# Down weights of the experts requested from ScalarE's queue, and the matmul order of the expert blocks

## The reference

```
hid = silu(xb @ w_gate_e[e]) * (xb @ w_up_e[e])     # 1024 -> 256
y   = hid @ w_down_e[e]                             # 256 -> 1024
```

## Time and profile before

| what | us |
|---|---|
| three runs, median (lowest to highest) | 2059.25 (2058.33 to 2060.5) |
| profiled execution, device time | 2059.05 |
| profiled execution, span | 2056.0 |

### The profile page before, as it was taken

One profiled execution on the slowest core, in us unless ns is written; L12 is line 12 of the kernel. 1 busy time (PEld: TensorE's weight loads), 2 busy tenths in 40 slices (PEclk: granted clock), 3 DMA queues, 4 the chain that ended last, 5 costly groups with the idle time before them and its releaser, 6 DMA issues.

```text
span 2056.0 us, 23309 instructions
## 1 busy us (share of the span) xinstructions
PE 1977.9 (96%) x9524; PEld 1411.7 (69%) x9524; DVE 1004.5 (49%) x1599; ACT 746.0 (36%) x1283; POOL 220.5 (11%) x271
## 2 busy tenths in 40 slices
PE   7999999999999999999999999999999998988888
PEld 6877788888888888888888886678886333323233
DVE  4376533445766642568988738664434211111113
ACT  5343332234444431466555533662333111111110
POOL 2000000002000000201112114110011221111100
PEclk9999999999999999999999999999999999999999
DMA  7331222243222242323332221112279999999998
GB/s 265 106 123 62 79 86 82 103 148 129 103 103 89 96 144 103 131 86 108 128 118 95 94 103 62 42 62 103 101 317 338 416 409 421 421 421 421 422 423 331
DMA packets 64059, 379.90 MB, mean 185 GB/s; under 512 B 13624, under 2 KB 13880, under 8 KB 32464
## 3 DMA queue, kind: packets, MB, share of 16 engines
q1 hardware_dynamic: 45792, 339.23, 42.8%
q0 software_dynamic: 17584, 38.09, 5.3%
q10 hardware_dynamic: 576, 1.09, 0.2%
HBM read 377.80 MB, written 27.89 MB: 197 GB/s over the span
## 4 chain that ended last, share of the span: by engine, by line
PE 76%; DMA 14%; DVE 5%; ACT 1%; SPq 1%; POOL 1%; issue 1%; DVEq 0%; POOLq 0%; ACTq 0%
PE PS L534 19%; PE PS L535 18%; PE PS L536 18%; DMA AR<-in_wexp 12%; PE PS L1301 6%; PE PS L995 3%; PE PS L1330 2%; SPq L3132 1%; DMA AR<-x2d 1%; PE PS L900 1%; DVE AR L1753 1%; PE PS L1047 1%; PE PS L1077 1%; PE PS L1279 1%; DVE rf L1379 1%
## 5 line engine op out<-in xcount | busy, mean ns | idle before, releaser
L534 PE MATMUL PS<-rf,rf 128*128 128x512 f32 (+1 forms) x1944 | 752.8, 387 | 5.3 <-DVE rf L1379 5.3
L536 PE MATMUL PS<-rf,rf 128*128 128x512 f32 (+1 forms) x1944 | 741.9, 382 | 0.0
L535 PE MATMUL PS<-rf,rf 128*128 128x512 f32 (+1 forms) x1944 | 741.2, 381 | 0.0
L1379 DVE TENSOR_TENSOR rf<-AR,rf 128x1024 fp32r<-128x1024 f32 (+1 forms) x228 | 286.0, 1260 | 335.2 <-ACT rf L2321 335.2
L534 PEld LDWEIGHTS PS<-rf,rf 128*128 128x128 f32 x1944 | 366.3, 188 | 81.8 <-DVE rf L1379 7.3
L536 PEld LDWEIGHTS PS<-rf,rf 128*128 128x128 f32 x1944 | 366.0, 188 | 70.6
L535 PEld LDWEIGHTS PS<-rf,rf 128*128 128x128 f32 x1944 | 366.6, 189 | 68.1 <-issue 1.2
L2321 ACT ACTIVATE rf<-AR 128x1024 fp32r<-128x1024 f32 (+1 forms) x228 | 245.2, 1084 | 258.1 <-PE PS L536 202.9
L1301 PE MATMUL PS<-AR 128*64 128x512 f32 x1012 | 266.2, 635 | 48.2 <-DMA AR<-in_wexp 47.9
L1301 PEld LDWEIGHTS PS<-AR 128*64 128x64 f32 x1012 | 81.8, 146 | 222.7 <-issue 154.5
L2246 DVE COPY AR<-PS 128x256 f32<-128x256 f32 x32 | 13.6, 425 | 316.1 <-PE PS L1313 316.1
(11 more groups left out here) (349 smaller groups left out, 1802.4 us busy)
## 6 DMA issues: line engine op xcount, KB each, us to landing
AR<-in_wpack SPq DMA_DIRECT2D x123, 1024.0 KB, 5.0
AR<-in_wexp SPq DMA_DIRECT2D x64, 1024.0 KB, 32.3
AR<-in_wexp SPq DMA_DIRECT2D x28, 2048.0 KB, 33.4
AR<-in_wexp SPq DMA_DIRECT2D x26, 1536.0 KB, 32.1
AR<-in_wexp SPq DMA_DIRECT2D x63, 512.0 KB, 20.9
AR<-acud POOLq DMA_DIRECT2D x16, 512.0 KB, 4.8
AR<-ya SPq DMA_DIRECT2D x4, 1024.0 KB, 8.2
bvec<-bv POOLq DMA_DIRECT2D x1, 2560.0 KB, 16.0
```

What stands on the lines that cost most here:

```text
L534: e.i.matmul(o, ws[0], xs[0], start=start, stop=False)
L535: e.i.matmul(o, ws[0], xs[1], start=False, stop=False)
L536: return e.i.matmul(o, ws[1], xs[0], start=False, stop=stop)
L1379: e.i.tensor_tensor(rounded(p.place + p.width, p.width), src, rounded(p.place, p.width).bitcast(F32), ALU.subtract).then_inc(*tick("w_lo", ...
```

## The change

Four things change.

1. Down weights of experts 6 to 63 are no longer in SP's list. ACT asks for them: after it has evicted block b (`rows_out`, L2866) it issues the two transfers for block b + 3, each 1 MB. SP keeps gate/up weights (and down weights of experts 0 to 5).
2. These transfers count on semaphores of their own (`da`), for which `downs` waits.
3. From block 2 on PE no longer runs gates one block ahead: the order is `gates(b)`, `turned_rows(b+1)`, `hidden(b)`, `downs(b)`. Blocks 0 and 1 are written out before the loop.
4. DVE's and ACT's programs are put in the same order.

```
+                if blk + 3 < NBLK:
+                    for n in (2 * blk + 6, 2 * blk + 7):
+                        e.i.dma_start(area(DNs[n % 6], 2048), wexp[n, :, 4096:6144]).then_inc(*tick(f"da{n % 6}", n, 16))
...
-            for blk in range(END - 2):
-                gates(blk + 1)
-                hidden(blk)
-                turned_rows(blk + 2)
-                downs(blk)
-            hidden(END - 2)
-            downs(END - 2)
-            for blk in (END - 1, END):
+            gates(1)
+            hidden(0)
+            turned_rows(2)
+            downs(0)
+            hidden(1)
+            downs(1)
+            for blk in range(2, NBLK):
                 if blk == END:
                     overflow(e, tensor_more, before_end)
                 gates(blk)
-                if blk < END:
-                    turned_rows(END)
+                if blk + 1 < NBLK:
+                    turned_rows(blk + 1)
                 hidden(blk)
                 downs(blk)
...
             def downs_in(n):
-                if n < 6:
-                    e.wait_ge(*at(*DN_FREE[n]))
-                else:
-                    e.wait_ge(*at("acc", ("dn2", n // 2 - 3, 1)))
+                e.wait_ge(*at(*DN_FREE[n]))
                 expert_in(f"dn{n % 6}", n, n, area(DNs[n % 6], 2048), 4096)
...
-                if blk > 3:
-                    downs_in(n - 2)
-                    downs_in(m - 2)
-            for x in range(2 * END - 4, 2 * END - 2):
-                downs_in(x)
...
-            downs_in(n)
-            downs_in(m)
```

More of the change, by code:

```diff
@@ L1327, in downs @@
                             n = 2 * blk + j
-                            e.wait_ge(*at(f"dn{n % 6}", n))
+                            e.wait_ge(*at(f"dn{n % 6}" if n < 6 else f"da{n % 6}", n))
                             w = cut(area(DNs[n % 6], 2048), 2)
@@ L2263, in vector @@
             over()
-            for blk in range(NBLK):
+            hidden_out(0)
+            hidden(1)
+            turned_rows(2)
+            rows_out(0)
+            hidden_out(1)
+            over_slots()
+            rows_out(1)
+            for blk in range(2, NBLK):
                 if blk == END:
                     overflow(e, vector_more, before_end)
[L2267 to L2270, removed]
+                hidden(blk)
+                if blk + 1 < NBLK:
+                    turned_rows(blk + 1)
                 hidden_out(blk)
[L2272 to L2276, removed]
                 rows_out(blk)
```

## The result

| kernel | runs | median us (lowest to highest) | ratio to before (95% interval) |
|---|---|---|---|
| before | 15 | 2057.88 (2055.25 to 2060.5) | |
| changed | 15 | 2064.47 (2061.91 to 2068.76) | 1.0033 (1.0026 to 1.0041) |

The changed kernel is 6.6 us slower by the medians. Its profiled execution took 2063.24 us, with a span of 2061.4 (before: 2056.0), so the two profiles lie 5.4 us apart. The forecast was 2068, +9.

What follows compares the result with a forecast made beforehand. Bytes through full DMA engines were taken to set the pace, the end by block 30's gate weights. +10.55 - 0.56 - 0.6 = +9.4, taken as +9 on 2059.05: 2068, range 2061 to 2076.

Steps and rivals of the forecast that it cites:

- rival A: DMA queues served in order of issue: 6 MB behind block 30's gate weights, gates(30) at 2017.9, +4, 2063; chance 0.13.
- Engines full, bytes and rate unchanged: Expert stage: DMA share 1.01 at 419 GB/s as before, last weight landing at 2033.7 again.
- Rival D: The two queues together move 1 to 2 per cent less: +13 to +18, 2072 to 2077; chance 0.11.
- A queue of its own brings the down weights early: ACT's queue is served beside SP's deep one; down weights land about 10 to 16 us after issue.
- Rival B: Who asks for a transfer makes no difference, block 30's gate weights land as now: 2059; chance 0.09.
- Only gate(31) behind gate(30): At the end, 4 of 8 MB remain behind block 30's gate weights: landing 2023.15 instead of 2012.6, +10.55.
- Gates(30) at full clock: Block 30's gate matmuls may take 7.08 instead of 8.78 us; a third of the 1.7 taken, -0.6.
- The gather of 31 stays hidden: Block 31's rows land by 2026.4, needed at 2030.2 or later: 4 us to spare, 0.56 wait gone.
- PE free before gate(30) lands: After block 29, PE is free at 2021.7, before block 30's gate weights land: no cost.
- The order costs 0.6 a block where PE is the bound, 0 here: Uncovered hidden chain makes PE's block 12.3 instead of 11.7, below the 15.75 of the transfers: worth 0.
- ACT's issues hidden: ACT's 58 added issues, at 0.33 to 0.8 us each, are hidden before its next instruction.
- Rival C: SP's queue gets over two thirds of the bytes, down weights fall behind: -2.6, 2056.5; chance 0.09.

Runs made afterwards that it cites:

- queue-alone run: Kernel before with down weights from expert 6 on asked for by ACT, old order of PE, DVE and ACT kept: 1.0054, 2069.65 us.
- order alone: Kernel before with only the new order of PE, DVE and ACT, all down weights staying in SP's list: 1.0001, 2058.74 us.
- the last run: Changed kernel with down weights of blocks 28 to 31 in SP's list, each behind its own block's gate weights: 0.9996, 2057.38 us.

## Why the prediction was right, and where it was off

The likeliest mechanism came: slower, through the later landing of block 30's gate weights. The size was off. +6.6 was measured (+5.4 between the profiles), where the sum's own ends were +8.3 and +10.0; 2064.5 lies in the range, which began below rival A's 2063, and it is nearer to A's number than to 2068. Gates(30) at 2020.33 are outside the 2021 to 2025 given as the sign and above the 2019 that would have meant A or C. So the number alone could not tell the forecast from A; the landing times do. Step by step:

- *Engines full, bytes and rate unchanged.* Right: 417 and 419 GB/s. Rival D (two queues move less) is out. The last weight landed at 2032.2 for 2033.7. About 0.8 of these 1.5 us is probably the start: POOL's first load of `x2d` is issued at 1503.60 instead of 1504.38, before anything that the change touches. The rest is open.
- *A queue of its own brings the down weights early.* Right: 12.2 us to landing, forecast 10 to 16, while SP's transfers of 2 MB take 37.6. So the queues are not served in order of issue, and rival A is out. Rival B is out too: the rate stayed, as by its rule, but not the time. And the runs with two or three blocks' down weights in SP's list show that this order of arrival is the cause.
- *Only gate(31) behind gate(30)*, half of 21.1 us, gates(30) at 2023.15. This term was too large: 2020.33, so 2.8 us less. 1.5 of it is the earlier last landing. The other 1.3 is the stretch from gates(30) to the last landing: 11.9 us and not 10.55. What lay behind was indeed only gate(31). The last two down transfers landed at 2022.1, 17.0 us after their issue and not 12, but from 2020.3 to 2033.0 ACT's queue moved only 0.05 MB more:

```profile
q1 hardware_dynamic: 877, 3.17, 61.9%
q10 hardware_dynamic: 9, 0.05, 1.0%
```

The halving was the error. At the end the engines do not stop together, and this tail does not shrink with the bytes. Windows of before, then of after:

```profile
2029.00:2033.70 4.70, 4.70 (x24) 1.90 (x22) 0.00 (x0) 0.00 (x0) 0.98 (x1) 1.00 0.45 176
2027.00:2032.20 5.20, 4.68 (x26) 2.12 (x26) 2.07 (x4) 1.52 (x5) 0.00 (x0) 1.00 0.37 149
```

The DMA share is 0.45 and 0.37 over the last 4.7 and 5.2 us. Only the part before it became shorter, 16.4 to 6.7 us at 402 and 395 GB/s.

- *Gates(30) at full clock: -0.6 of a possible 1.7.* Mis-sized: it was the whole 1.69. The granted clock was 1.00 from 2020.3 to 2027.4 in the changed kernel and 0.72 from 2012 to 2018 in the kernel before (0.50 from 2013 to 2016), so part of the latter ran at the lower of the two levels (1.2 GHz); with 1.51 us of idle before them in place of 2.21, gates(30) took 7.09. With the 0.56 of the gather this closes the sum.
- *The gather of 31 stays hidden.* Right, with 2.2 us to spare instead of 4: issued at 2018.64, landed at 2025.1, needed at 2027.3. The prediction named that downs(28) now come before gates(29), but priced the new order at 0. The queue-alone run shows that with the old order PE waits 5 us for the gather.
- *PE free before gate(30) lands: no cost.* Right for the changed kernel, by 1.5 us. As a rule it was too narrow: in the runs with down weights of one, two or three blocks back in SP's list the last wait sat at gates(29), (28) and (27).
- *The order costs 0.6 a block where PE is the bound, 0 here.* Right: 0.7, and 0.0 (order alone).
- *ACT's issues hidden*: right at 0.39 us; at rows of 2 KB they no longer are, and there they make most of the loss.

Rival C (down weights fall behind) was taken as the faster side. With the 4 KB rows they fall behind, and the kernel is slower than before. The reasoning of C counted only the end and forgot the waits for down weights in the blocks (10 of them from 1700 to 1990).

## What to carry to other kernels

Here transfers filled the engines, and giving one kind a queue of its own did not change the rate (419 GB/s) but the order of arrival: the short queue overtook the long one (12.2 against 37.6 us to landing). Look for this wherever a kernel is bound by its transfers. Load last what is used last; early weights for a late stage push back those that the critical stage waits for, and the bill comes at the end. That bill is not bytes over rate alone: the last 5 us of transfers ran at a DMA share under one half, in both kernels. So look at the last blocks as sums, landing of block b's weights plus PE's work after it, and take the largest over b, not only the last. And where an edit has two parts, run each alone: here one was free and the other cost 11 us, and together they cost 6.6.

## What the runs showed of the hardware that was not expected

- A wait can cost more than its length. The gates of a block take 7.04 to 7.07 us when PE hasn't idled, and 8.78 in the changed kernel at 1990.40 after 3.13 us of idle (granted clock 0.57 from 1990 to 1994), in the last run at 2013.79 after 2.79. But 2.93 us of idle in the earlier trace rows was followed by 7.08. What decides was not settled.
- Two queues with the same 62 MB in ACT's: with rows of 4 KB instead of 8 KB the rate stays nearly the same (416 for 419 GB/s) while ACT's transfers fall behind. With rows of 2 KB single issues hold ACT for up to 11.6 us and a block's eight for 18.68, and PE's waits behind that (64.1 us) are the larger part of the loss. The mean rate there, 381 GB/s, is that of a stretch with pauses, and no rate for rows of 2 KB.
- When the list of transfers ends, the rate falls over some 5 us (176 and 149 GB/s on the mean), in both kernels.
